# A merging stage's three projections as float32r parts, with loads in the order of their use

## What is computed

```python
merged = (sigmoid(g_fox + b_gate[:D]) * (out_fox @ w_proj_fox)      # out_fox, out_dsa: 1024 x 512
          + sigmoid(g_dsa + b_gate[D:]) * (out_dsa @ w_proj_dsa))   # weights 512 x 1024 each
x = x + gt1 * (merged @ w_out)                                       # w_out 1024 x 1024
h2 = rmsnorm(x, norm2_g) * (1 + sc2) + sh2
y = hierarchical_moe(h2, router weights, 32 experts, top 2)          # routing, then the experts
x = x + gt2 * y
```

## Time and profile before

| | us |
|---|---|
| runs: median (lowest to highest) of 3 | 3400.55 (3399.44 to 3404.88) |
| the profiled execution, its own time | 3398.51 |
| its span | 3396.3 |
| PE busy | 2863.1 (84%) |
| DVE busy | 2118.6 (62%) |
| ACT busy | 1235.3 (36%) |
| mean granted TensorE clock | 0.912 of full |

### The profile page before, as it was taken

One profiled execution on the slowest core, in us unless ns is written; L12 is line 12 of the kernel. 1 busy time (PEld: TensorE's weight loads), 2 busy tenths in 40 slices (PEclk: granted clock), 3 DMA queues, 4 the chain that ended last, 5 costly groups with the idle time before them and its releaser, 6 DMA issues.

```text
span 3396.3 us, 34380 instructions
## 1 busy us (share of the span) xinstructions
PE 2863.1 (84%) x12552; PEld 2126.6 (63%) x12552; DVE 2118.6 (62%) x2906; ACT 1235.3 (36%) x2024; POOL 535.3 (16%) x320
## 2 busy tenths in 40 slices
PE   7999959979588699879889958795988479999992
PEld 3777746755466444468767847684444368888882
DVE  6399945526688523344726979841222479999985
ACT  3122221110366511122224126572211067777772
POOL 1422100000111100001200045452110011111101
PEclk9999979989788799989999969897999689999996
DMA  6333237534455432134442164114324289999995
GB/s 204 102 103 109 88 130 257 192 127 137 164 187 177 159 135 75 44 112 119 114 122 72 72 144 89 26 41 169 117 75 157 97 316 412 416 412 414 412 389 217
DMA packets 259104, 586.24 MB, mean 173 GB/s; under 512 B 27189, under 2 KB 158245, under 8 KB 241650
## 3 DMA queue, kind: packets, MB, share of 16 engines
q1 hardware_dynamic: 185618, 449.00, 36.9%
q0 software_dynamic: 29968, 64.18, 6.4%
q10 hardware_dynamic: 43344, 70.79, 5.6%
HBM read 463.26 MB, written 120.65 MB: 172 GB/s over the span
## 4 chain that ended last, share of the span: by engine, by line


## 5 line engine op out<-in xcount | busy, mean ns | idle before, releaser
L2413 DVE TENSOR_TENSOR e_low<-e_raw,e_high 128x4096 fp32r<-128x4096 f32 x99 | 438.0, 4426 | 69.5 <-ACT e_high L2407 69.4
L2407 ACT ACTIVATE e_high<-e_raw 128x4096 fp32r<-128x4096 f32 x99 | 359.5, 3633 | 32.8 <-DVE live L2364 26.4
L128 PE MATMUL banks<-p_w_high,p_high 128*128 128x512 f32 (+1 forms) x640 | 250.1, 391 | 18.1 <-DVE p_w_low L1526 18.1
L128 PE MATMUL banks<-p_w_low,p_high 128*128 128x512 f32 (+1 forms) x640 | 245.8, 384 | 0.0
L128 PE MATMUL banks<-p_w_high,p_low 128*128 128x512 f32 (+1 forms) x640 | 245.1, 383 | 0.0
L128 PE MATMUL banks<-c_w,c_mT 128*128 128x512 f32 x512 | 225.9, 597 | 9.0 <-DMA c_w<-in_w_out 9.0
L128 PE MATMUL banks<-e_high,e_xhigh 128*128 128x512 f32 x528 | 211.1, 400 | 10.0 <-issue 7.2
L483 DVE SCALAR_TENSOR_TENSOR acc<-img,taps,acc 128x1024 f32<-128x1024 f32 x160 | 209.8, 1311 | 5.7
L128 PE MATMUL banks<-h_high,w_high 128*128 128x512 f32 (+1 forms) x544 | 201.0, 370 | 9.2 <-POOL w_low L355 4.5
L128 PE MATMUL banks<-e_high,e_xlow 128*128 128x512 f32 x528 | 207.9, 394 | 0.0
L128 PE MATMUL banks<-e_low,e_xhigh 128*128 128x512 f32 x528 | 207.2, 392 | 0.0
(11 more groups left out here) (452 smaller groups left out, 6127.5 us busy)
## 6 DMA issues: line engine op xcount, KB each, us to landing
e_raw<-in_exp_w SPq DMA_DIRECT2D x99, 2048.0 KB, 10.6
mod_w<-in_ada_w SPq DMA_DIRECT2D x24, 1024.0 KB, 6.1
s_sums<-cumT SPq DMA_DIRECT2D x32, 768.0 KB, 5.2
s_X<-xtok SPq DMA_DIRECT2D x19, 1024.0 KB, 7.4
p_raw<-in_w_in SPq DMA_DIRECT2D x18, 1024.0 KB, 6.5
y<-e_y ACTq DMA_DIRECT2D x33, 512.0 KB, 10.9
xbcT<-res ACTq DMA_DIRECT2D x20, 640.0 KB, 2.9
xtok<-xt ACTq DMA_DIRECT2D x20, 640.0 KB, 3.7
```

Source lines behind the costliest of these rows:

```text
L128: last = pe.matmul(out, a, b, start=start and n == 0, stop=stop and n == len(pairs) - 1)
L2407: act.activation(self.high[p % HIGHS][:], self.raw[p % RAWS][:], ACT.Copy).then_inc(*self.high_done.up())
L2413: dve.tensor_tensor(self.low[p % HIGHS][:], self.raw[p % RAWS][:], self.high[p % HIGHS][:].bitcast(F32), ALU.subtract).then_inc(*self.low_ ...
```

## The change

- The three projections are computed as three float32r products each. The weights are loaded raw and split: high parts (`m_wp_high`, `m_wo_high`) by ScalarE into own buffers, low parts by VectorE in place, over the raw ones. The attention outputs are split in the same way (`m_oT_high` one buffer, `m_oT_low` two), and the turned merged tile into `m_mT_high` and `m_mT_low` straight from PSUM.
- The gated products are written over the gates (`m_gs`), and `m_x` and `m_h` serve for several of the former buffers; x has one buffer and is loaded after the x2 store of the tile before.
- The loads stand in another order: GpSimd issues `m_oT` first and the weights in eight pieces of 1 MB; SP issues gates and bias first, and the rest after the fourth piece.
- The experts' raw buffers come after `merge`; their first three pieces are fetched at the head of `route`.

Core of the diff:

```diff
+    def both(self, name, shape):
+        with self.core.nc.sbuf_tensor(name + "_raw", shape, F32) as raw:
+            pass
+        return raw, self.sb(name, shape, R32)
...
-        pool.dma_start(wp[0][:], weights("w_proj_fox_2")).then_inc(*weights_in[0].up())
-        pool.dma_start(wp[1][:], weights("w_proj_dsa_2")).then_inc(*weights_in[1].up())
-        pool.dma_start(wo[:], weights("w_out_2")).then_inc(*weights_in[2].up())
...
+        def split_weights(n):
+            hi, lo, raw = (a[:, n % KD, :] for a in ((wph, wpl, wp_raw) if n < KD else (woh, wol, wo_raw)))
+            act.wait_ge(*w_in[n // 2].at(1))
+            act.activation(hi, raw, ACT.Copy).then_inc(*w_high.up())
+            dve.wait_ge(*w_high.at(n + 1))
+            dve.tensor_tensor(lo, raw, hi.bitcast(F32), ALU.subtract).then_inc(*w_split.up())
...
+        def split_o(t):
+            b = t % 2
+            act.wait_ge(*o_in[b].at(2 * (t // 2) + 2))
+            for j in range(2):
+                hi, lo, raw = (a[:, 4 * j:4 * j + 4, :] for a in (oh, ol[b], o_raw[b]))
+                if t:
+                    act.wait_ge(*projected.at(2 * t - 1 + j))
+                act.activation(hi, raw, ACT.Copy).then_inc(*o_high.up())
+                dve.wait_ge(*o_high.at(2 * t + j + 1))
+                dve.tensor_tensor(lo, raw, hi.bitcast(F32), ALU.subtract).then_inc(*o_low.up())
...
         def bring_x(t):
+            if t:
+                sp.wait_ge(*x2_stored.at(t))
+                sp.wait_ge(*h_done.at(t))
+            sp.dma_start(x[:], dram["x1"][P * t:P * t + P, :]).then_inc(*x_in.up())
...
-                for half in range(2):
-                    last = products(pe, core.bank[:, 2 * j + half, :], [(oT[b][:, 4 * j + k, :], wp[j][:, k, 512 * half:512 * half + 512]) for k in range(4)])
+                for k in range(4 * j, 4 * j + 4):
+                    if t == 0:
+                        pe.wait_ge(*w_split.at(k + 1))
+                    for half in range(2):
+                        last = products(pe, core.bank[:, 2 * j + half, :], three(oh[:, k, :], ol[b][:, k, :], *(a[:, k, 512 * half:512 * half + 512] for a in (wph, wpl))),
+                                        start=k == 4 * j, stop=k == 4 * j + 3)
...
+            for q in range(2):
+                src = turn(q, gs[t % 2], m_turned)
+                hi, lo = (a[:, 4 * q:4 * q + 4, :] for a in (mh, ml))
+                act.activation(hi, src, ACT.Copy).then_inc(*m_high.up())
+                dve.wait_ge(*m_high.at(2 * t + q + 1))
+                dve.tensor_tensor(lo, src, hi.bitcast(F32), ALU.subtract).then_inc(*m_low.up())
+            bank_free.append(m_low.now())
...
-        bring(0), bring_x(0)
+        bring_o(0)
+        for j in range(8):
+            load_weights(j)
+        split_o(0)
+        for n in range(KD):
+            split_weights(n)
+        bring_g(0)
+        sp.wait_ge(*w_in[3].at(1))
+        bring_x(0), bring_rows()
...
             if n + 1 < NT:
-                bring(n + 1)
+                bring_o(n + 1), bring_g(n + 1), split_o(n + 1)
...
+            if n == 0:
+                for k in range(KD, 2 * KD):
+                    split_weights(k)
...
-        route(core, dram, tables)
+        route(core, dram, tables, lambda: [weights.fetch(m, j, m) for m, j in weights.order[0:3]])
```

More of the change, by code:

```diff
@@ L2105, in merge @@
[L2105 to L2111, removed]
@@ L2113, in merge, with bring_rows, prepare_gain @@
+        def bring_rows():
+            for to, of in ((gate, mod[2 * D:3 * D]), (gain, dram["norm2_g_2"]), (h, mod[4 * D:5 * D]), (shift, mod[3 * D:4 * D])):
+                sp.dma_start(to[:], row(of)).then_inc(*rows_in.up())
+        def prepare_gain():
+            dve.wait_ge(*rows_in.at(4))
+            dve.scalar_tensor_tensor(out=gain[:], in0=h[:], scalar=1.0, in1=gain[:], op0=ALU.add, op1=ALU.mult).then_inc(*vec.up())
+            dve.wait_ge(*vec.now())
         flat = lambda j: flat2(core.bank[:, 2 * j:2 * j + 2, :])
+        turn_bank = lambda q: core.bank[:, 6 + q, :]
@@ L2114, in merge @@
         bank_free = []
[L2116 to L2124, removed]
@@ L2126, in bring, with turn, bring_o @@
-        def bring(t):
+        def turn(q, src, turned):
+            if bank_free:
+                pe.wait_ge(*bank_free[-1])
+            turns(pe, [(turn_bank(q)[:, P * j:P * j + P], src[:, 512 * q + P * j:512 * q + P * j + P]) for j in range(4)], ident).then_inc(*turned.up())
+            act.wait_ge(*turned.now())
+            return turn_bank(q).rearrange("p (j n) -> p j n", j=4)
+        def bring_o(t):
             b, at = t % 2, slice(P * t, P * t + P)
             if t >= 2:
-                sp.wait_ge(*projected.at(2 * t - 2))
+                pool.wait_ge(*projected.at(2 * t - 2))
@@ L2197, in close @@
                 dve.wait_ge(*h_turned.at(2 * t))
-            dve.scalar_tensor_tensor(out=h[:], in0=x2[:], scalar=norm.rs[:, 0:1], in1=gain[:], op0=ALU.mult, op1=ALU.mult).then_inc(*vec.up())
+            dve.tensor_tensor(h[:], flat(2), gate[:], ALU.mult).then_inc(*scaled.up())
+            dve.wait_ge(*scaled.at(t + 1))
+            dve.wait_ge(*x_in.at(t + 1))
+            dve.tensor_tensor(x[:], x[:], h[:], ALU.add).then_inc(*x2_done.up())
+            act.wait_ge(*x2_done.at(t + 1))
+            act.dma_start(dram["x2"][at, :], x[:]).then_inc(*x2_stored.up())
+            dve.wait_ge(*x2_done.at(t + 1))
+            norm.rstd(x[:], eps)
+            dve.scalar_tensor_tensor(out=h[:], in0=x[:], scalar=norm.rs[:, 0:1], in1=gain[:], op0=ALU.mult, op1=ALU.mult).then_inc(*vec.up())
             dve.wait_ge(*vec.now())
@@ L2207, in turn_normed @@
             pe.wait_ge(*h_done.at(t + 1))
-            turn(hT, h, h_turned, h_copied)
+            for q in range(2):
+                src = turn(q, h, h_turned)
+                act.activation(hT[:, 4 * q:4 * q + 4, :], src, ACT.Copy).then_inc(*h_copied.up())
+            bank_free.append(h_copied.now())
         def router(t):
             if t == 0:
-                pe.wait_ge(*weights_in[3].at(2))
+                pe.wait_ge(*router_in.at(2))
             pe.wait_ge(*h_copied.at(2 * t + 2))
@@ L2230, in merge @@
                 close(n - 1)
-            if n + 1 < NT:
-                bring_x(n + 1)
+            if 0 < n < NT:
+                bring_x(n)
             if n == NT - 2:
@@ L2693, in late @@
     with Stage(core) as s:
-        weights = Weights(core, s, dram)
         nought, emptied, spills_cleared = s.sb("e_nought", [P, 256]), s.sem("e_emptied"), s.dma("e_spills_cleared")
         def look_ahead():
-            for m, j in weights.order[0:3]:
-                weights.fetch(m, j, m)
             sp.wait_ge(*emptied.at(1))
```

92 lines of the change are left out of this document (47 added, 45 removed).

## The result

| | before | after |
|---|---|---|
| median of 4 runs (lowest to highest), us | 3400.63 (3399.44 to 3404.88) | 3369.96 (3363.43 to 3372.27) |
| profiled execution, its own time | 3398.51 | 3368.75 |
| its span | 3396.3 | 3367.0 |
| PE busy | 2863.1 | 2822.6 |
| DVE busy | 2118.6 | 2163.7 |

The changed kernel is faster: the ratio is 0.9904, 95% interval 0.9887 to 0.9922. The forecast was 3355 with a range of 3346 to 3370, so the time lies at the very end of the range (two of the four runs lie outside it), and two thirds of the forecast gain of 45.7 us came.

The account below looks back on a forecast made before the run. The head was taken as bound by DMA, later tiles by TensorE's pace. Gains of 9.4 (head), 5.1 (tile 1), 29.0 (tiles 2 to 6) and 2.2 (tile 7) sum to 45.7 us: median 3355, range 3346 to 3370.

Parts of the forecast that it names:

- The head: Start of the merging stage: gates ready just before tile 1's attention outputs, tile 0's end 9.4 us earlier.
- The rule weighed: Head's loads: queues take turns by whole packets, so short rows get long ones' share; would make the median 3353; not used.
- Tile 1: Merging stage, second tile: interval 29.2 us less 5.8 for faster products, gates' chain 0.7 late; 5.1 us won.
- Tiles 2 to 6: Steady merging stage: period 38.1 to 32.3 us by two faster product groups, idle 4.94 stays; 29.0 us in five periods.
- Tile 7: Last merging tile: one product group gives 2.9 us, the turn of h waits 0.7 longer; 2.2 us won.
- Routing: Seam to the experts: early fetch of three pieces lies in idle DMA time; 0 us, up to 1 of cost.
- The sum: Whole kernel: 9.4 + 5.1 + 29.0 + 2.2 = 45.7 us won, median 3355.
- (a): Head gives nothing: router's short rows on SP's queue hold back tile 1's gates; 3364; with milder forms 0.22.
- (c): Steady tiles slower: TensorE isn't granted the high clock, 123 us more, 3478; chance 0.04.
- (d): Steady tiles: the gates' path sets the period, which stays 38.1 us; 3393 to 3400; chance 0.04.
- (b): Head gives more: tile 2's gates don't get ahead of tile 1's outputs, and restarts are shorter; 3349; chance 0.08.

Follow-up runs that it names:

- the swap: Changed kernel with the split of a tile's attention outputs put ahead of its gates' bias and sigmoid in ScalarE's order: 3355.83 us, ratio to before 0.9868.

## Why the prediction was nearly right, and where it failed

- **The head (9.4 us forecast, 1.1 came).** This is the step that failed: "Its gates are in by about 2378 ... 2384.4, just before". I let the gates come first and the outputs last, at +45.5. It was the other way round: outputs at +38.8, gates at +42.6. I had given SP's ring its 3.5 MB between 2360.5 and 2378, some 210 GB/s; it had 150 of 389. Since the high copy stands on ScalarE behind the sigmoid, the late gates held up an operand that was there; the swap alone gives 9.9 us of tile 0's end back, 11.9 of TensorE's time. The second part of the step, 0.6 us for the low part, was 4.05 because I looked at VectorE's own duration and not at what GpSimd did beside it: 3.5 us of tile 0's end, by the run in which the bias waits. The two can't be added: the swap mends both.
- **The rule weighed.** The outputs came 6.7 us sooner than my sum made them, but this doesn't speak for turns by whole packets. My 16.4 million bytes put both gates loads ahead of the outputs. These are 2.1 million bytes, 5.4 us at 389 GB/s, and they landed behind them, at +42.6 and +45.1; the 1 us that I added for short rows is about the rest (an estimate). The Trainium skill (DMA: Bandwidth & Descriptors, section Queues, rings and completion order) states the turns by packets, but no share of bytes for short rows; the 1 or 2 us were my reading of it, and no run here tests it.
- **Tile 1 (5.1 forecast, 5.2 came).** The size is right by luck. I had the gates' chain 0.7 us late; it is 1 us early: VectorE waits 0.98 us for `close`'s last product in that tile, so TensorE sets the 23.98. Two slower groups (next point) make up for the 0.7.
- **Tiles 2 to 6 (29.0 forecast, 25.6 came).** The mechanism was right (idle 4.92 stands, two groups of 48), a size was off: the period is 33.0 instead of 32.3. In the timeline `close` takes 11.4 us (13.9 before) instead of 11.0, so each group gives 2.5 us and not 2.9. A product takes 0.232 us here, from start to start in the mean, against 0.228 in the experts and my 0.226 from ten steps; that is 0.3 of the 0.4 us. The rows:

```profile
2465.68 0.40 PE L134 MATMUL banks<-m_wp_high,m_oT_high 128*128 128x512 f32 x1
...
2467.78 0.39 PE L134 MATMUL banks<-m_wp_high,m_oT_high 128*128 128x512 f32 x1
```

  Nine steps are 2.10 us. The group with the restart varies from 12.8 to 14.1, 13.5 in the mean, where I had 13.2; its restart costs the same 2.1 us as before, so here too it is the pace. Together this is the 0.7 us a period, more than the 0.5 that I had given as a bound, for the restart alone.
- **Tile 7 (2.2 forecast, 2.5 came).** Right.
- **Routing (0 forecast, with up to 1 of cost; 1.2 came as a cost).** The cost lies just over my bound: the fetch delays the row of counts.
- **The sum.** In place of 9.4 + 5.1 + 29.0 + 2.2 the stage gave 1.1 + 5.2 + 25.6 + 2.5 = 34.4, less 1.2 of routing 33.2. The medians differ by 30.7, which the interval of the ratio (26.5 to 38.4 us) covers; the profiled spans by 29.3, where the later start of the stage takes 4.5. With all of it the median lies 0.04 us inside the range, and its own runs reach from 3363.4 to 3372.3: that it is inside and not outside is luck.
- **The rivals.** (a) had the time nearest to the result of all, 3364, and the right chain: the gates come behind the outputs, and bias, sigmoid and split set the first product (at +53.8; it had +56 for the end of the split). Its cause falls: the router's small rows do hold up SP for 10.56 us, but with them on the other ring the gates land as late. (c) didn't happen, and the run with ScalarE's logits shows its other side: the low clock comes from the idle 4.92 alone and goes with it. (d) didn't happen: the sigmoid is in time in every tile from 2 on. Of (b) the first half came true, as even tile 1's gates came behind the outputs, and it gave nothing, since the split stands behind the sigmoid.
- **What I passed by.** The 4.94 us of waiting stood in my own period as a constant. A wait of TensorE for a copy of 128x36 at the end of another engine's chain was worth more (35.8 us) than the whole change.

## What to carry to other kernels

- A split put between a load and a product makes the in-order queue of the splitting engine part of the product's path. Put it ahead of everything there that waits for other data; list for each operand what stands before its copy, and when that one's data land.
- When the sum has a steady wait of TensorE in it, price its removal first, with the restart at 1.2 GHz behind it: 4.92 us of idle time cost 7.2 a tile.
- For every VectorE operation with two operands in SBUF that is to be on the path, look what GpSimd does at that time; where loads of two queues are in flight together, bound each queue's share from both sides instead of giving it half.

## What the runs showed of the hardware that was not expected

- One GpSimd addition of 128x2048 (4.5 us) holds up a VectorE operation with two SBUF operands until it ends (2.2 to 3.4 us lost in the rows above), and two in a row hold up a pair for 8.2 (9.51 against 1.29). VectorE's record shows the delay as busy time, not as a wait. Operations that read one operand from PSUM aren't held up (1.2 us each beside the same GpSimd addition).
- SP took 10.56 us to issue the router's 128 KB in runs of 128 bytes, where GpSimd took 0.92 for the same transfer. The short runs aren't shown to be the reason: the kernel before has an issue of 7.34 us for gates, whose rows are long, behind other loads on the same ring.

```profile
2345.02 7.34 SPq L2134 DMA_DIRECT2D m_gs<-proj  x1
```

  The 10.56 us cost nothing here, since the ring had loads to move.
- A float32r product of 128x512 takes 0.232 us in the merging stage and 0.228 in the experts, at the full granted clock in both. The order of banks isn't the reason; it stays open.
- Where TensorE had no idle time the granted clock was 1.00 of full over 80 us, where it waited 4.92 us in each tile it was 0.91.
